# Two-layer decoder trunk on one core: inputs laid out turned by the host, an opening with six weight places, memory values in natural order, one PSUM bank swapped

## The reference

```
layer 0:  z = x @ a_w_in                      # 1024 x 1792: 768 for u, 768 for v, 256 memory queries
          mix = chunked_sgu(gelu(u), layer_norm(gelu(v)), a_w_s, a_b_s)   # causal 128x128 gates, 12 heads
layer 1:  mix = fox_attention(q, k_sh, v_sh, logcum)                      # 12 heads, forget gates
both:     mkv = mem @ mem_w_kv[layer]         # 256 memory tokens: 256 columns of keys, 256 of values
          mo  = memory_attention(qm, mk, mv)  # 4 heads of 64
          y = concat([mix, mo]) @ w_o[layer]
          x = layer_norm(ALPHA * x + y)
          x = layer_norm(ALPHA * x + square(relu(x @ w_up)) @ w_down)
```

## Time and profile before

| | us |
|---|---|
| median of 3 runs | 1187.76 |
| lowest and highest of them | 1186.54 and 1188.23 |
| the profiled execution, own time | 1186.62 |
| its span in the profile | 1184.9 |
| PE busy (share of the span) | 1154.3 (97%) |
| DVE / ACT / POOL busy | 632.8 / 489.2 / 135.7 |

### The profile page before, as it was taken

The page is one execution under the profiler, slowest core; times in us unless marked ns, Lnnn a source line. Parts: engine busy times, 40 slices in busy tenths (PEclk is TensorE's granted clock), DMA queues, the critical chain, the costliest instruction groups (busy, mean ns, idle before and its releaser), DMA issues.

```text
span 1184.9 us, 16507 instructions
## 1 busy us (share of the span) xinstructions
PE 1154.3 (97%) x5840; PEld 970.4 (82%) x5840; DVE 632.8 (53%) x1080; ACT 489.2 (41%) x847; POOL 135.7 (11%) x156
## 2 busy tenths in 40 slices
PE   7989999999999999999999999999999999999997
PEld 7877789888888888889878888789888888888886
DVE  5667566644332444345578777866454323454226
ACT  5446236543211334224675555636543212333220
POOL 4200034200000000133400001035100000000000
PEclk9999999999999999999999999999999999999999
DMA  6521232333333333332311222123233333233232
GB/s 215 145 71 54 72 107 73 89 106 89 107 90 106 89 91 105 97 98 72 89 36 55 71 69 55 54 84 96 75 101 92 104 97 98 87 90 102 94 107 89
DMA packets 185591, 107.22 MB, mean 90 GB/s; under 512 B 4482, under 2 KB 180162, under 8 KB 185540
## 3 DMA queue, kind: packets, MB, share of 16 engines
q1 hardware_dynamic: 183236, 101.04, 29.3%
q10 hardware_dynamic: 2304, 5.51, 1.4%
HBM read 104.43 MB, written 2.10 MB: 90 GB/s over the span
## 4 chain that ended last, share of the span: by engine, by line
PE 80%; DVE 8%; ACT 4%; issue 4%; DMA 2%; POOL 1%; ACTq 0%; DVEq 0%; SPq 0%; POOLq 0%
PE proj L535 65%; PE pv L535 3%; PE sc L535 3%; DVE w_lo L1490 2%; PE proj L891 2%; PE tr L891 2%; PE pv L891 2%; PE tr L582 2%; PE sc L891 1%; ACT w_hi L1106 1%; DMA w_raw<-in_w_down 1%; ACT x L1276 1%; DMA mem_nat<-in_mem 1%; POOL total L2091 1%; DVE sc L1552 1%
## 5 line engine op out<-in xcount | busy, mean ns | idle before, releaser
L1490 DVE TENSOR_TENSOR w_lo<-w_raw,w_hi 128x1024 fp32r<-128x1024 f32 x171 | 217.8, 1273 | 164.6 <-ACT w_hi L1106 116.4
L535 PE MATMUL proj<-x_hi,w_hi 128*128 128x512 f32 (+1 forms) x768 | 300.3, 392 | 1.9 <-DVE w_lo L1490 0.7
L535 PE MATMUL proj<-x_hi,w_lo 128*128 128x512 f32 (+1 forms) x768 | 294.9, 385 | 0.0
L535 PE MATMUL proj<-x_lo,w_hi 128*128 128x512 f32 (+1 forms) x768 | 289.7, 384 | 0.0
L1106 ACT CAST w_hi<-w_raw 128x1024 fp32r<-128x1024 f32 x158 | 165.1, 1045 | 203.6 <-PE proj L535 197.9
L535 PEld LDWEIGHTS proj<-x_hi,w_hi 128*128 128x128 f32 x768 | 145.6, 190 | 30.2 <-ACT x_hi L1278 1.8
L535 PEld LDWEIGHTS proj<-x_hi,w_lo 128*128 128x128 f32 x768 | 145.5, 190 | 29.1
L535 PEld LDWEIGHTS proj<-x_lo,w_hi 128*128 128x128 f32 x768 | 143.1, 189 | 25.4
L535 PE MATMUL proj<-h_hi,w_hi 128*128 128x512 f32 (+1 forms) x384 | 146.4, 381 | 0.4 <-DVE w_lo L1490 0.4
L535 PE MATMUL proj<-h_hi,w_lo 128*128 128x512 f32 (+1 forms) x384 | 146.0, 380 | 0.0
L535 PE MATMUL proj<-h_lo,w_hi 128*128 128x512 f32 (+1 forms) x384 | 146.0, 380 | 0.0
(11 more groups left out here) (356 smaller groups left out, 1795.0 us busy)
## 6 DMA issues: line engine op xcount, KB each, us to landing
w_raw<-in_w_up SPq DMA_DIRECT2D x64, 512.0 KB, 4.0
w_raw<-in_w_down SPq DMA_DIRECT2D x64, 512.0 KB, 3.6
w_raw<-in_w_o SPq DMA_DIRECT2D x16, 512.0 KB, 3.6
w_raw<-in_a_w_in SPq DMA_DIRECT2D x14, 512.0 KB, 3.8
w_raw<-in_kv_w SPq DMA_DIRECT2D x12, 512.0 KB, 3.9
w_raw<-in_mem_w_kv SPq DMA_DIRECT2D x8, 512.0 KB, 4.5
w_raw<-in_b_w_q SPq DMA_DIRECT2D x8, 512.0 KB, 3.6
x_nat<-in_x ACTq DMA_DIRECT2D x2, 1024.0 KB, 11.6
```

Source lines behind the costliest of these rows:

```text
L535: last = pe.matmul(target, lhs, rhs, start=start and n == 0, stop=stop and n == len(terms) - 1)
L1490: return dve.tensor_tensor(target, whole, hi.bitcast(F32), ALU.subtract)
```

## The change

The host hands over `x`, `mem` and the gate matrices already transposed, the weights of `a_w_in` and `mem_w_kv` as contiguous units, and the layer norm parameters turned (`norms`). So PE's transposes of `mem` (twice), `x`, the gate matrices and the parameters go, with DVE's copies of `x`. Units 0 to 5 have a raw place each, and their loads wait for no split. The first unit comes in halves, and PE begins with 20 matmuls on ones. DVE takes the rests of tiles 3, 5 and 7 of `x`, POOL keeps five. The memory values are projected with memory tokens as stationary operand and both value units as moving one, so that they come out in natural order; their transposes go. In the bank table `Z_BANK` the v tiles 4 and 5 change places.

```diff
+    OPEN = 6
+    X_REST = [3, 5, 7]
+    WARM = 20
+    Z_BANK = [0, 1, 0, 1, 1, 0]
...
+        def raw(b):
+            if b.trip is None and 2 <= b.base < OPEN:
+                return open_raw[:, b.base - 2]
+            return w_raw[:, b.slot]
...
         def space(b):
+            if b.trip is None and b.base == B_AQ:
+                return B_AQ
...
-            memory_weights(0, range(4))
-            for c in range(MEMPAIRS):
-                load(Pos(B_AQ + c), cols(a_w_in[0], 2 * DMIX + c * P))
+            for c in range(2):
+                part = slice(c * KT // 2, (c + 1) * KT // 2)
+                sp.dma_start(w_raw[:, 0, part], mem_w_kv[0, 0][:, part]).then_inc(first_landed[c], 16)
+            sp.wait_ge(mem_landed[0], 16)
...
+            memory_weights(0, range(1, 4))
+            for c in range(2):
+                quarter(c)
+            load(Pos(B_AQ), a_w_in[2 * PAIRS])
+            for c in range(2, 4):
+                quarter(c)
+            load(Pos(B_AQ + 1), a_w_in[2 * PAIRS + 1])
...
-            def memory_values(layer):
-                for c in range(2, 4):
-                    g = Pos(G_MEM[layer][c])
-                    pe.wait_ge(proj_free[g.slot], g.half(2))
-                transposes(Pos(T_MV[layer]), [v_tmp[:, c, m * P:(m + 1) * P] for m in range(MT) for c in range(2)])
+            def memory_values(layer, m, parts=(0, KT)):
+                b, g = Pos(B_MEM[layer][2]), Pos(G_MEM[layer][2 + m])
+                here = slice(m * P, (m + 1) * P)
+                bank = proj[g.slot][:, 0:M].rearrange("p (c n) -> p c n", c=2)
+                for k in range(*parts):
+                    if k == 0:
+                        pe.wait_ge(w_split, b.at(2))
+                        wait(pe, proj_free[g.slot], g.half())
+                    mh, ml = mem_hi[layer][:, k, here], mem_lo[layer][:, k, here]
+                    wh, wl = w_hi[:, :, k, :], w_lo[:, :, k, :]
+                    last = products(bank, [(mh, wh), (mh, wl), (ml, wh)], k == 0, k == KT - 1)
+                if parts[1] == KT:
+                    last.then_inc(w_used, 1)
...
                 if s.trip is None and s.base < STEP_B:
-                    pe.wait_ge(z_out, (1, 2, 5, 4)[2 * s.base + head])
+                    pe.wait_ge(z_out, (1, 2, 3, 5)[2 * s.base + head])
...
-            for n in range(3):
-                project(Pos(B_AU + 2 + n), Pos(G_AU + 2 + n), x_hi, x_lo)
-                transposes(Pos(T_WS + n), [ws_raw[:, h] for h in range(4 * n, 4 * n + 4)])
-            project(Pos(B_AU + 5), Pos(G_AU + 5), x_hi, x_lo)
+            for n in range(2, PAIRS):
+                project(Pos(B_AU + n), Pos(G_AU + n), x_hi, x_lo)
...
+            def memory_values(layer, m):     # DVE: the rest of the values, and the bank's release
+                g = G_MEM[layer][2 + m]
+                dve.wait_ge(mv_hi_ready, MT * layer + m + 1)
+                rest(mv_lo[:, m], proj[g % 2][:, 0:M], mv_hi[:, m]).then_inc(proj_free[g % 2], 1)
...
                     prepare(Pos(B_BQ))
-                    finish(n, 1, {2: (lambda: prepare(Pos(B_BQ + 1)),)})
+                    finish(n, 1, {1: (lambda: memory_values(1, 0),), 2: (lambda: prepare(Pos(B_BQ + 1)),), 4: (lambda: memory_values(1, 1),)})
```

More of the change, by code:

```diff
@@ L64, in trunk_kernel @@
 def trunk_kernel(nc, x, mem, a_w_in, a_sgu_ln_g, a_sgu_ln_b, a_w_s, a_b_s, kv_w, kv_b_f, b_w_q,
[L65 to L67 removed]
+                 mem_w_kv, w_o, ln_g, ln_b, norms, w_up, w_down, out):
+    _, T, D = out.shape
+    M = mem.shape[2]
     KT = D // P
@@ L449, in load @@
             def load(b, source):
-                wait(sp, w_split, b.at(-1))
+                if b.trip is None and b.base < OPEN:
+                    sp.dma_start(raw(b), source).then_inc(landed(b)[0], 16)
+                    return
+                wait(sp, w_split, b.base - OPEN + 1 if b.trip is None and b.base < OPEN + 2 else b.at(-1))
                 sp.dma_start(w_raw[:, b.slot], source).then_inc(w_landed[b.slot], 16)
@@ L589, in transposes, with first_projection @@
                 turned(tr[t.slot], pieces).then_inc(tr_done, 1)
-            def memory_transposes(layer, n):
-                pe.wait_ge(mem2_landed if layer else mem_landed[n // 2], 16)
-                if layer:
-                    pe.wait_ge(tr_free, T_MEM[1] + n - 1)
-                turned(mem_bank[layer][n], [mem_in[layer][:, m, k * P:(k + 1) * P]
-                                            for k in (2 * n, 2 * n + 1) for m in range(MT)]).then_inc(tr_done, 1)
+            def first_projection():
+                bank = proj[0][:, 0:M]
+                for half in range(2):
+                    tiles = range(half * KT // 2, (half + 1) * KT // 2)
+                    pe.wait_ge(w_hi_ready if half else first_hi, 1)
+                    for k in tiles:
+                        if k % 2 == 0:
+                            pe.wait_ge(mem_hi_ready, k // 2 + 1)
+                        pe.matmul(bank, w_hi[:, 0, k], memt_hi[:, k], start=k == 0, stop=False)
+                    pe.wait_ge(w_split if half else first_lo, 1)
+                    for k in tiles:
+                        pe.matmul(bank, w_lo[:, 0, k], memt_hi[:, k], start=False, stop=False)
+                    for k in tiles:
+                        if k % 2 == 0:
+                            pe.wait_ge(mem_split, k // 2 + 1)
+                        last = pe.matmul(bank, w_hi[:, 0, k], memt_lo[:, k], start=False, stop=k == KT - 1)
+                last.then_inc(w_used, 1)
             def memory_projection(layer, c, parts=(0, KT)):
@@ L2156, with turned, units @@
     from concourse.bass_utils import run_bass_kernel_spmd
+    def turned(a):
+        return a.T.reshape(-1, P, a.shape[0]).transpose(1, 0, 2)
+    def units(w):
+        *front, d, n = w.shape
+        return np.moveaxis(w.reshape(*front, d // P, P, n // P, P), (-2, -3, -4), (-4, -3, -2))
+    laid = dict(inputs)
+    laid["x"], laid["mem"] = turned(inputs["x"][0]), turned(inputs["mem"][0])
+    laid["a_w_in"], laid["mem_w_kv"] = units(inputs["a_w_in"][0]), units(inputs["mem_w_kv"])
+    laid["a_w_s"] = inputs["a_w_s"][0].transpose(2, 0, 1)
+    laid["norms"] = np.concatenate([inputs["ln_g"].reshape(-1, P), inputs["ln_b"].reshape(-1, P)]).T
     nc = bacc.Bacc("TRN2", target_bir_lowering=False, num_devices=1)
@@ L2160 @@
     for name in _INS:
-        a = np.ascontiguousarray(inputs[name])
+        a = np.ascontiguousarray(laid[name])
         arrays[f"in_{name}"] = a
```

236 lines of the change are left out of this document (117 added, 119 removed).

## The result

| | before | after |
|---|---|---|
| median, us | 1188.23 | 1197.23 |
| lowest to highest (11 runs each) | 1186.54 to 1189.51 | 1190.50 to 1199.30 |
| time ratio, 95% interval | | 1.0062 [1.0046, 1.0078] |
| profiled execution: time, span | 1186.62, 1184.9 | 1199.30, 1197.6 |
| its mean granted clock | 0.994 | 0.983 |

The ratio is not the quotient of the two medians, which is 1.0076: the medians differ by 9.0 us. The forecast was 1186.2, with a range up to 1190.3; the median lies 11 us above it. The runs of the changed kernel follow their mean clock: 1190.5 us at 0.991, 1193.6 and 1194.6 at 0.988, 1195.6 to 1199.3 at 0.982 to 0.985.

What follows compares the result with a forecast made beforehand. The prediction took PE to bound the kernel, busy 1154.3 of 1184.9 us. Its gains and losses, including -4.0 for clock falls, summed to 1.6 us saved: 1187.76 - 1.6, about 1186.2, range 1182.0 to 1190.3.

Runs made afterwards that it cites:

- e5: Kernel before with the z-tile bank swap, plus only gate matrices, parameters and layer 1's mem laid out turned by the host: 1185.65 us.
- e7: Kernel before with the bank swap, plus unread matmuls in four waits (three in layer 0's output projection, one at layer 1's first probabilities): 1181.65 us.
- e1: The swap alone: kernel before with only the banks of z tiles 4 and 5 exchanged; 1184.61 us.
- e14: Kernel before, bank not swapped, with 13 unread matmuls inside PE's 3.28 us wait for z tile 4: 1184.69 us.
- e6: Kernel before with the bank swap, plus only layer 1's memory values projected in natural order: 1188.07 us.
- e8: Changed kernel with unit 1's load issued right behind unit 0, plus unread matmuls in its waits: 1187.81 us.

## What to carry over

A wait of PE costs its own length and, behind it, up to 1.7 us for each stretch at half clock. When a change takes PE's work away where another engine sets the pace, the work comes back as waiting, and here the waiting was dearer than the transposes (e5 stands 1.0 us above the swap alone): take it away only where PE arrives late. Before moving a load, look at what is in flight beside it, not at the landing of a lone one. And where a wait can't be removed, matmuls that nobody reads are worth trying: 25 of them (e7) gained 3.0 us on top of the swap.

## What the hardware showed beyond that

- **The clock is not decided by the length of one wait.** The same 1.99 us at the first probabilities were followed by a stretch at half clock in the profiled run of before and of e5, and by none in e1 and e14. Executions of one kernel differ along with their clock: those of e6 by 8.6 us.
- **The start.** In the changed kernel 20 matmuls on ones end at 5.8 us, PE waits 1.99, and the first projection then runs at 0.215 us per 256 columns to its end, although the granted clock reads 1.00. In e8, where 28 of them leave no gap, the groups of four take 1.05 us up to 10.3, and 0.63 from 11.1 on:

```profile
9.42 1.05 PE L648 MATMUL proj<-memt_lo,w_hi 128*128 128x256 f32 x4
11.12 0.63 PE L644 MATMUL proj<-memt_hi,w_lo 128*128 128x256 f32 x4
```

- **DVE beside POOL.** With both inputs in SBUF 1024 columns take 3.10 us in place of 1.23, and POOL is slowed too: in the changed kernel its sums of 512 columns took 1.28 us at best, and 2.21 and 1.74 from 173.3 on, beside a split and a rest of DVE. In the kernel before the same two sums took 2.21 and 1.74 as well, beside two splits and a shift of DVE.
